# Two transformer blocks in split fp32 on one core: deviations per token, the Fourier step in two turns, and three steps moved in the order

## The chip, the cores and the metric

One core of one Trainium2 chip runs the whole program in one launch. The metric is the device time of an execution in microseconds; of several executions the median counts. The engines are TensorE (PE; its weight load is PEld), VectorE (DVE), ScalarE (ACT), GpSimd (POOL) and SyncE (SP), which issues the weight DMAs.

## The reference

A first block (attention, a recurrent mixer and four gated FFNs, two layers deep) is followed by a second block, also two layers, with a mixer and a convolutional FFN in each. There are 256 latent tokens and 256 context tokens, 1024 features, 2816 hidden features in an FFN. Layer 1 of either block needs the latent tokens alone from its queries on. What the change touches:

```
def second_block(...):
    for l in range(2):
        a = modulate(rms_norm(h, g_mix), sh1, sc1)
        h = h + gt1 * mixer(a)
        h = h + gt2 * conv_ffn(modulate(rms_norm(h, g_ffn), sh2, sc2))
    return rms_norm(h_x, g_final)

def mixer(h):
    fa = real(fft2(reshape(h @ w_fa, tokens, 4, 128)))         # over tokens and 128 features
    o  = softmax(q1 k1) v - lam * softmax(q2 k2) v             # 4 heads of 128
    db = o * rsqrt(mean(o*o, last axis) + 1e-5) * subln_g * (1 - lam_init)
    nc = neighbourhood_attention(...)                          # 8 heads of 64
    g_a, g_b, g_c = split(sigmoid(h @ w_g + b_gate), 3)
    return (g_a * (fa @ w_a) + g_b * (db @ w_b) + g_c * (nc @ w_c)) @ w_out

def conv_ffn(h):
    a, b = split(dwconv3(h @ w_up), 2)                         # 3 taps along the tokens
    return (silu(a) * b) @ w_down
```

## The kernel before

Activations lie with features on the partitions: X holds 8 chunks of 128 features x 512 tokens (latent 0 to 255, context 256 to 511). Each large product is made of three matmuls per 128x128 tile: both operands are split into a high half, rounded to fp32r, and a low half, what is left (HH and HL for activations, a pair of slots in WR for weights); hi*hi, hi*lo and lo*hi are summed in one of eight banks. Weights come in slabs of up to 1 MB into three ring buffers; `split` makes a slab's high half on ScalarE (a Copy of 128x2048) and its low half on VectorE (a subtraction), into one of three pair slots (two in the mixers of attention). The ring buffer is loaded again once the low half is done.

One list, ORDER, holds every step. Each engine's program walks through it and takes its own share of a step, so the list sets the order on every engine; semaphore waits tie them together. `woven` merges lists evenly. A planner at the end puts each slab's split as early as its pair slot allows, two slabs ahead at most; in the first group of a projection, and where ORDER says `split_next`, other rules hold. The steps that matter here, with the functions that write them:

- `lin` is a projection in groups of four output chunks with K = 8 in two slabs: `slab` (one output chunk's matmuls with one slab) and `ev` (eviction of a bank). A slab step takes 12 matmuls. `first_group` runs the first group of a projection chunk by chunk behind the norm (`times`, `mod_h`, `mod_l`, the last of which makes HL); for 512 tokens it has two halves, and for 256 tokens (the last FFN of the first block, called 11, and the conv FFN of layer 1) one.
- `lin_deep` is an FFN's second product, K = 22: `part` copies a chunk of the hidden activations to HH (ScalarE) and subtracts into HL (VectorE), eight chunks at a time in the places where the first product's operand lay. Before the first of them `warm` makes ScalarE load the Sqrt table. `part` 0 waits for the last matmul of the first product. In the conv FFN an eviction is an Identity with scale and bias on ScalarE, two taps on VectorE, a Silu on ScalarE and a product on VectorE.
- `mixer2` (second block): projections and the difference attention `da`; `da_rest`, its deviations, woven into the first fifth of the gate projection; the neighbourhood attention `na`; eight `sig` (sigmoids of the first gate, in place); the second gate woven with the Fourier step; the first, second and third mix (gate times fa @ w_a and so on, into YM); `y_parts`, which splits YM for the last projection `mo`.
- `da_rest` has per head: `hsum` (Square on ScalarE, a matmul with a 128x128 tile of ones, and scale and add on VectorE over all tokens), `hroot` (Sqrt, reciprocal) and `db_norm` (the product).
- `fourier` (l, g, sg) has two matmuls with the 128-point table, VectorE's two copies to UC (one of two buffers, by the number n = 2g + sg), four matmuls with the 256-point tables, ScalarE's copy to the high half and VectorE's subtraction. There are eight in layer 0 and four in layer 1, where all numbers are even.

In the first block `head_sq`, `head_sum`, `head_root` and `head_spread` do the same as da_rest in another form: sums per token into a few columns of one bank, root and reciprocal of these few columns, and a matmul that spreads each column over its partitions.

Of the kernel before, what the change touches and what calls it, by code (L numbers as in the profile page):

```python
# [10 lines left out]
ALU = mybir.AluOpType  # L11
ACT = mybir.ActivationFunctionType
AXX = mybir.AxisListType.X
P = 128
# [5 lines left out]
EPS = 1e-6  # L20
# [140 lines left out]
def program(nc, A, out):  # L161
    ctx = ExitStack()
    with ctx:
# [233 lines left out]
        def first_group(J):  # L397
# [7 lines left out]
            for k in range(K):  # L405
                chunk(k + 2, 0)
                ORDER.append(("slab_k", J, k // 4, k, 0))
                if halves == 2:
# [10 lines left out]
                    if k >= 6:  # L419
                        chunk(k - 6, 1)  # L420
            if halves == 2:
# [88 lines left out]
        HEAD = {"eqk": (0, 5, 0, 1.0 / 64, EPS), "kk": (40, 4, 5, 1.0, EPS), "read": (0, 4, 9, 1.0 / 64, GN_EPS)}  # L510
# [32 lines left out]
        def even_mixer(mods0, mods1):  # L543
# [14 lines left out]
            for name, w0, w1 in (("eqk", 0, 7), ("kk", 6, 14)):  # L558
                n = HEAD[name][1]
# [47 lines left out]

        def head_rstd(name, src, dst, n, width, scale, eps, group):
            for m in range(n):
                ORDER.append(("hsum", name, m, src(m), dst(m), width, scale, eps, group))  # L610
            for m in range(n):
                ORDER.append(("hroot", name, m, dst(m)))
# [141 lines left out]
        MRS = wv(XTRA, [4, 512])  # L754
# [21 lines left out]
        def mixer2(l):  # L776
# [190 lines left out]
        def tensor_program(e, q):  # L967
# [182 lines left out]
            def hsum(name, m, src, dst, width, scale, eps, group):  # L1150
                q.wait_ge(IN["cst"], ("in", "cst"))
                q.wait_ge(ACTS, ("hsq", name, m))
                o = take(("hsum", name, m))
                mm(o[:, 0:width], C(group), SQ[m % 2][:, 0:width], True, True).then_inc(
                    MM.sem, MM.mark(("hsum", name, m)))
                shut(("hsum", name, m))

# [9 lines left out]
            def head_sum(name, m):  # L1167
                o0, n, i0, *_ = HEAD[name]
# [3 lines left out]
                q.wait_ge(ACTS, ("head_sq", i0 + m))  # L1172
# [1235 lines left out]
```

## Time and profile before

| | |
|---|---|
| timed runs | 3922.23, 3925.08, 3933.41 us; median 3925.08 |
| profiled execution | 3916.84 us; its span 3915.0 us |
| mean granted clock of TensorE | 0.965 |
| TensorE, weight loads | 3598.5 us (92%), 2964.7 us (76%) |
| VectorE, ScalarE, GpSimd | 1895.7 (48%), 1388.0 (35%), 60.1 us (2%) |
| DMA | 453.93 MB, mean 116 GB/s |

A row of the timeline gives the start and the duration in us, the engine, the line of the kernel (988 is the helper of every matmul, 1209 the transposes, 1422 every activation, 1742 to 1757 VectorE's helpers), the operation, out<-in, the shape, and how many alike were merged; in brackets the engine's idle time just before and what ended it. Layer 0 of the second block's mixer runs from about 2340 to 2885 us of the span, layer 1's from about 3330 to 3685.

### The profile page before, as it was taken

What the parts mean: (1) busy time and instruction counts of PE and PEld (TensorE: products, weight loads), DVE (VectorE), ACT (ScalarE), POOL (GpSimd) and SP (SyncE); (2) the same over time, 40 slices, a digit from 0 to 9 for tenths busy, and PEclk for the clock granted to TensorE, in tenths of its full rate; (3) what the DMA queues carried; (4) which work ended last, traced back from release to release, by engine and by line L of the source; (5) the groups of instructions that cost most, each with busy time, mean ns of one, the idle gap of its engine ahead of it and who ended that gap; (6) DMA issues with size and microseconds to landing.
All of it is one profiled execution on the core that took longest, in us unless ns stands there. A gap on an engine that the chain in (4) does not pass through costs nothing.

```text
span 3915.0 us, 61954 instructions
## 1 busy us (share of the span) xinstructions
PE 3598.5 (92%) x27214; PEld 2964.7 (76%) x27214; DVE 1895.7 (48%) x3248; ACT 1388.0 (35%) x2195; POOL 60.1 (2%) x98
## 2 busy tenths in 40 slices
PE   6999999888889999999987979988999999988798
PEld 4777874777668888878756978656887778778798
DVE  2223455777754233323465444662454443564574
ACT  3213435322233233323334343442243333344453
POOL 0000000000010000000000000010000000010000
PEclk8999999999999999999998989999999999999899
DMA  5444224222243322333145542121225542233453
GB/s 188 173 164 140 76 63 145 89 99 99 88 96 96 97 92 84 119 129 123 61 162 178 185 144 76 60 60 54 87 86 180 184 159 79 97 97 108 134 178 109
DMA packets 257918, 453.93 MB, mean 116 GB/s; under 512 B 14096, under 2 KB 157584, under 8 KB 243184
## 3 DMA queue, kind: packets, MB, share of 16 engines
q1 hardware_dynamic: 253840, 441.68, 33.7%
q0 software_dynamic: 3808, 8.27, 1.3%
q8 instruction: 215, 3.52, 0.4%
q14 instruction: 55, 0.45, 0.0%
HBM read 447.24 MB, written 1.94 MB: 115 GB/s over the span
## 4 chain that ended last, share of the span: by engine, by line
PE 78%; DVE 13%; ACT 5%; DMA 2%; issue 2%; SPq 0%; POOL 0%; DVEq 0%; ACTq 0%; POOLq 0%
PE bank L988 77%; DVE WR L1742 2%; DVE W L1751 2%; DVE W L1742 2%; ACT W L1422 2%; ACT WR L1422 2%; PE bank L1209 1%; DVE W L1754 1%; DVE H L1742 1%; DVE HL L1742 1%; DVE X L1751 1%; DMA ring<-in_w_mod 1%; DMA ring<-in_w_ada 1%; DVE small L2005 1%; ACT H L1422 0%
## 5 line engine op out<-in xcount | busy, mean ns | idle before, releaser
L988 PE MATMUL bank<-HH,WR 128*128 128x512 f32 (+1 forms) x9312 | 2430.7, 348 | 94.1 <-DVE HL L1742 46.5
L988 PEld LDWEIGHTS bank<-HH,WR 128*128 128x128 f32 x9312 | 1647.8, 193 | 352.0 <-DVE HL L1742 57.9
L988 PE MATMUL bank<-HL,WR 128*128 128x512 f32 (+1 forms) x4656 | 1603.8, 344 | 0.0
L1742 DVE TENSOR_TENSOR WR<-ring,WR 128x2048 fp32r<-128x2048 f32 (+3 forms) x300 | 674.0, 2252 | 1181.1 <-ACT WR L1422 1181.1
L1422 ACT ACTIVATE WR<-ring 128x2048 fp32r<-128x2048 f32 (+3 forms) x300 | 562.5, 1881 | 1235.5 <-PE bank L988 837.5
L988 PEld LDWEIGHTS bank<-HL,WR 128*128 128x128 f32 x4656 | 898.6, 193 | 97.8 <-issue 0.7
L1422 ACT ACTIVATE W<-bank 64x256 f32<-64x256 f32 (+3 forms) x582 | 259.2, 449 | 482.1 <-PE bank L988 440.4
L988 PE MATMUL bank<-W 64*64 64x64 f32 (+5 forms) x6304 | 366.6, 252 | 59.7 <-ACT W L1422 20.4
L988 PEld LDWEIGHTS bank<-W 64*64 64x64 f32 (+3 forms) x6304 | 277.2, 144 | 152.9 <-issue 53.7
L1422 ACT ACTIVATE W<-bank,small 128x512 f32<-128x512 f32 (+2 forms) x183 | 113.0, 621 | 261.1 <-DVE small L2005 178.4
L1754 DVE COPY W<-bank 64x256 f32<-64x256 f32 (+3 forms) x352 | 135.2, 396 | 108.6 <-PE bank L988 103.9
L1742 DVE TENSOR_TENSOR W<-W,bank 128x512 f32<-128x512 f32 (+1 forms) x140 | 82.9, 597 | 180.0 <-PE bank L988 179.8
L1751 DVE SCALAR_TENSOR_TENSOR W<-bank,vec,W 128x510 f32<-128x510 f32 (+1 forms) x206 | 130.6, 634 | 79.0 <-ACT W L1422 75.2
L988 PE MATMUL bank<-ring,silc 128*32 128x512 f32 x960 | 143.3, 643 | 23.0 <-DMA ring<-in_w_mod 16.3
L988 PE MATMUL bank<-cst,W 64*64 64x64 f32 (+6 forms) x1264 | 125.6, 266 | 32.1 <-DVE W L1754 22.2
L988 PEld LDWEIGHTS bank<-cst,W 128*128 128x128 f32 (+2 forms) x1264 | 107.7, 163 | 60.1 <-DVE W L1754 24.5
L1209 PE MATMUL bank<-cst,W 128*128 128x128 f32 x432 | 77.2, 295 | 38.1 <-DVE W L1746 33.5
L1209 PEld LDWEIGHTS bank<-cst,W 128*128 128x128 f32 x432 | 48.5, 146 | 81.1 <-issue 37.4
L1422 ACT ACTIVATE W<-bank,vec 128x512 f32<-128x512 f32 (+1 forms) x136 | 83.3, 628 | 59.9 <-PE bank L988 57.9
L988 PE MATMUL bank<-WR,HH 128*128 128x512 f32 (+2 forms) x384 | 102.8, 357 | 0.0
L1422 ACT ACTIVATE H<-H,MOD 128x256 f32<-128x256 f32 x144 | 86.1, 598 | 44.4 <-DVE H L1742 44.4
L1422 ACT ACTIVATE W<-W 128x512 f32<-128x512 f32 (+2 forms) x98 | 50.1, 532 | 145.5 <-DVE W L1751 91.8
(107 smaller groups left out, 2080.2 us busy)
## 6 DMA issues: line engine op xcount, KB each, us to landing
ring<-in_ffn_in SPq DMA_DIRECT2D x176, 512.0 KB, 5.0
ring<-in_w_mod SPq DMA_DIRECT2D x72, 1024.0 KB, 5.0
ring<-in_w_in SPq DMA_DIRECT2D x52, 1024.0 KB, 5.1
ring<-in_w_ada SPq DMA_DIRECT2D x48, 1024.0 KB, 6.5
ring<-in_ffn_out SPq DMA_DIRECT2D x176, 256.0 KB, 3.6
ring<-in_w_up SPq DMA_DIRECT2D x88, 512.0 KB, 5.1
ring<-in_w_down SPq DMA_DIRECT2D x88, 256.0 KB, 3.6
ring<-in_even_w_in SPq DMA_DIRECT2D x8, 1024.0 KB, 5.1
```

What stands on the lines that cost most here:

```text
L988: return e.matmul(o, l, r, start=start, stop=stop, skip_group_check=True)
L1209: x = e.transpose(o[:, c * P:(c + 1) * P], a["P"][j % 3][0][:, c * P:(c + 1) * P], C("ident"))
L1422: return e.activation(o, i, f, **kw).then_inc(ACTS.sem, ACTS.mark(*events))
L1742: put(e.tensor_tensor(o, a, b, op), *events)
L1751: put(e.scalar_tensor_tensor(out=o, in0=a, scalar=s, in1=b, op0=op0, op1=op1), *events)
L1754: put(e.tensor_copy(o, a), *events)
L2005: put(e.tensor_reduce(neg, bank[:, lo:nk], AXX, ALU.max, negate=True), ("neg", name, i, j))
```

## The change

- `da_rest` uses the head steps of the first block: sums per token (one column per head and 128 tokens), one root and reciprocal of 16 (layer 0) or 8 columns, and a spread per head; the steps hsum, hroot, db_norm and the tile MRS go.
- `fourier` becomes `fourier_a` (first product and copies) and `fourier_b` (second product and split); a of the next number stands ahead of b of this one, and the first a ahead of the gate projection. The buffer alternates by the count in both layers.
- The eight `sig` are woven among the gate projection's steps.
- In the third mix `y_parts` of a chunk comes after the eviction of the next.
- `lin_deep` puts parts 0 and 1 ahead of the last eviction of the first product, and `warm` behind them.
- `first_group` with one half (256 tokens) gets a `split_next` at k = 5, which splits the projection's third slab there.

```diff
 def lin_deep(name, wt, src, ntok, mod, idx, norm, ready):
-    ORDER.append(("warm",))
     J = Job(name, "deep", ...)
-    for k in range(4):
+    last = max(i for i, x in enumerate(ORDER) if x[0] == "ev")
+    ORDER[last:last] = [("part", J, k) for k in range(2)]
+    ORDER.append(("warm",))
+    for k in range(2, 4):
         ORDER.append(("part", J, k))
...
 # first_group, in the loop over k
                 if k >= 6:
                     chunk(k - 6, 1)
+            elif k == 5:
+                ORDER.append(("split_next",))
...
-HEAD = {"eqk": (0, 5, 0, 1.0 / 64, EPS), ...}
+HEAD = {n: dict(at=at, n=m, i0=i0, scale=scale, eps=eps, per=per, tok=tok) for ... in (
+    ("eqk", HN[:, 0:40], 5, 0, 1.0 / 64, EPS, 2, 4), ("kk", ...), ("read", ...),
+    ("db0", small[:, 36:52], 4, 13, 1.0 / P, 1e-5, 1, 4),
+    ("db1", small[:, 36:44], 4, 17, 1.0 / P, 1e-5, 1, 2))}
...
 def da_rest():
-    head_rstd(f"db{l}", lambda m: DB[:, m, 0:nq], lambda m: MRS[:, m, 0:nq], 4, nq, 1.0 / P, 1e-5, "ones")
+    n = f"db{l}"
+    ORDER.extend([("head_sq", n, 0), ("head_sq", n, 1), ("head_sum", n, 0), ("head_sq", n, 2), ("head_sum", n, 1),
+                  ("head_sq", n, 3), ("head_sum", n, 2), ("head_sum", n, 3), ("head_root", n)])
     for h in range(4):
-        ORDER.append(("db_norm", l, h, nq))
+        ORDER.append(("head_spread", n, h))
...
-for c in range(8):
-    ORDER.append(("sig", l, c, nq))
-woven(taken(lambda: gates(l, 1, nq, "gate")),
-      [("fourier", l, g, sg) for g in range(4) for sg in range(nq // 256)])
+ns = [2 * g + sg for g in range(4) for sg in range(nq // 256)]
+ORDER.append(("fourier_a", l, ns[0]))
+turns = []
+for i, n in enumerate(ns):
+    turns += [("fourier_a", l, x) for x in ns[i + 1:i + 2]] + [("fourier_b", l, n)]
+woven(taken(lambda: gates(l, 1, nq, "gate")), turns, [("sig", l, c, nq) for c in range(8)])
...
         if step[0] == "ev":
-            ORDER.append(("y_parts", l, 4 * step[1].kw["half"] + step[3], nq))
+            c = 4 * step[1].kw["half"] + step[3]
+            if c:
+                ORDER.append(("y_parts", l, c - 1, nq))
+    ORDER.append(("y_parts", l, 7, nq))
...
 # tensor engine, head_sum and head_spread
+ones = C("blk")... if per == 2 else C("ones", 0, 1)
+for t in range(tok):
+    c = per * (tok * m + t)
+    x = mm(banks[BANK["head", name]][:, c:c + per], src[:, t * P:(t + 1) * P], ones, True, True)
...
+for t, h in pairs(tok, per):
+    c = per * (tok * m + t) + h
+    x = mm(o[w * h:w * h + w, t * P:(t + 1) * P], d["at"][:, c:c + 1].to_broadcast([P, w]), C("ident"), True, True)
...
 # vector engine, head_spread of db and fourier_a
+stt(x, x, SUB, held(key)[:, 0:n], ALU.mult, ALU.mult, ("db", int(name[2]), m), ("free", key))
...
+UC = UCS[n // (1 + l) % 2]
+if n // (1 + l) >= 2:
+    q.wait_ge(MM, ("f2", l, n - 2 * (1 + l)))
```

## Rows read from the trace of the kernel before

**Rows 1.** the page: busy time, share of the span and instructions, by engine:
```profile
PE 3598.5 (92%) x27214; PEld 2964.7 (76%) x27214; DVE 1895.7 (48%) x3248; ACT 1388.0 (35%) x2195; POOL 60.1 (2%) x98
```

**Rows 2.** the page: chain that ended last, share of the span by engine:
```profile
PE 78%; DVE 13%; ACT 5%; DMA 2%; issue 2%; SPq 0%; POOL 0%; DVEq 0%; ACTq 0%; POOLq 0%
```

**Rows 3.** who TensorE waited for, whole span: total us, times, longest us:
```profile
PE bank L988 <- DVE HL L1742: 46.5, 20, 9.3
```

**Rows 4.** two windows: length, busy us by engine, PEclk, DMA share, GB/s:
```profile
2671.80:2675.30 3.50, 3.50 (x9) 2.83 (x9) 0.00 (x0) 0.00 (x0) 0.00 (x0) 0.51 0.83 294
3710.40:3716.30 5.90, 5.90 (x28) 5.90 (x29) 4.31 (x2) 0.69 (x1) 0.00 (x0) 0.50 0.83 259
```

**Rows 5.** timeline around both layers' deviations, TensorE and VectorE:
```profile
2535.05 1.02 PE L988 MATMUL bank<-W,cst 128*128 128x512 f32 x2
2536.71 12.98 DVE L1757 RECIPROCAL W<-W 128x512 f32<-128x512 f32 x4
2554.95 0.68 DVE L1742 TENSOR_TENSOR W<-W,cst 128x512 f32<-128x512 f32 x1
2559.36 1.09 PE L1209 MATMUL bank<-cst,W 128*128 128x128 f32 x4 [10.45 <-DVE W L1746]
...
3480.64 1.09 PE L1209 MATMUL bank<-cst,W 128*128 128x128 f32 x4 [6.08 <-DVE W L1746]
```

**Rows 6.** timeline, TensorE, a norm's sums per token and its spread over partitions:
```profile
2115.78 0.60 PE L988 MATMUL bank<-cst,W 128*128 128x1 f32 x4 [0.50 <-ACT W L1422]
2117.08 0.71 PE L988 MATMUL bank<-cst,small 128*128 128x128 f32 x4 [0.69 <-DVE small L1757]
```

**Rows 7.** TensorE's waits in the gate stages 2662 to 2745 and 3545 to 3592:
```profile
PE bank L988 <- DVE W L1754: 13.8, 8, 6.7
...
PE bank L988 <- DVE W L1754: 8.4, 4, 4.2
```

**Rows 8.** timeline, ScalarE and VectorE, start of layer 0's gate stage:
```profile
2662.60 4.27 ACT L1422 ACTIVATE W<-W 128x512 f32<-128x512 f32 x8
2668.70 2.29 DVE L1742 TENSOR_TENSOR WR<-ring,WR 128x2048 fp32r<-128x2048 f32 x1 [7.12 <-ACT WR L1422]
```

**Rows 9.** timeline, third mix and output projection, layer 0 and then layer 1:
```profile
2867.21 0.50 PE L988 MATMUL bank<-HH,WR 128*128 128x512 f32 x1 [2.33 <-DVE WR L1742]
...
3649.89 0.39 PE L988 MATMUL bank<-HH,WR 128*128 128x256 f32 x1 [3.64 <-DVE WR L1742]
3656.19 1.28 ACT L1422 ACT_TABLE_LOAD   x1
3656.21 0.42 DVE L1742 TENSOR_TENSOR HL<-W,HH 128x256 fp32r<-128x256 f32 x1 [0.48 <-ACT HH L1422]
3657.49 0.20 ACT L1422 ACTIVATE small<-small 128x1 f32<-128x1 f32 x1
3661.87 0.58 PE L988 MATMUL bank<-HH,WR 128*128 128x256 f32 x1 [4.48 <-DVE WR L1742]
```

**Rows 10.** timeline, start of the two conv FFNs' second matmul:
```profile
3183.87 1.52 DVE L1751 SCALAR_TENSOR_TENSOR W<-bank,vec,W 128x510 f32<-128x510 f32 x2
3186.56 3.69 DVE L1742 TENSOR_TENSOR HL<-W,HH 128x512 fp32r<-128x512 f32 x6
3187.39 0.77 PE L988 MATMUL bank<-HH,WR 128*128 128x512 f32 x1 [9.34 <-DVE HL L1742]
...
3834.10 0.55 PE L988 MATMUL bank<-HH,WR 128*128 128x256 f32 x1 [5.69 <-DVE HL L1742]
```

**Rows 11.** timeline, end of a first group of 256 tokens, twice:
```profile
2138.06 0.39 PE L988 MATMUL bank<-HH,WR 128*128 128x256 f32 x1 [3.88 <-DVE WR L1742]
...
3705.59 5.50 ACT L1422 ACTIVATE WR<-ring 128x2048 fp32r<-128x2048 f32 x3
3710.36 0.58 PE L988 MATMUL bank<-HH,WR 128*128 128x256 f32 x1 [8.77 <-DVE WR L1742]
```

**Rows 12.** the first group's stretch, columns as in rows 4:
```profile
2120.00:2134.00 14.00, 14.00 (x96) 13.97 (x96) 5.80 (x18) 6.84 (x13) 0.00 (x0) 0.80 0.00 1
```

More of the change, by code:

```diff
@@ L509, in program @@
         HN = wv(12032, [72])
-        HEAD = {"eqk": (0, 5, 0, 1.0 / 64, EPS), "kk": (40, 4, 5, 1.0, EPS), "read": (0, 4, 9, 1.0 / 64, GN_EPS)}
+        HEAD = {n: dict(at=at, n=m, i0=i0, scale=scale, eps=eps, per=per, tok=tok) for n, at, m, i0, scale, eps, per, tok in (
+            ("eqk", HN[:, 0:40], 5, 0, 1.0 / 64, EPS, 2, 4), ("kk", HN[:, 40:72], 4, 5, 1.0, EPS, 2, 4),
+            ("read", HN[:, 0:32], 4, 9, 1.0 / 64, GN_EPS, 2, 4), ("db0", small[:, 36:52], 4, 13, 1.0 / P, 1e-5, 1, 4),
+            ("db1", small[:, 36:44], 4, 17, 1.0 / P, 1e-5, 1, 2))}
         EF_ORDER = [range(4, 8), range(0, 4), range(8, 12), range(12, 15)]
@@ L1171, in head_sum @@
                 q.wait_ge(IN["cst"], ("in", "cst"))
-                q.wait_ge(ACTS, ("head_sq", i0 + m))
-                src = X1[m] if name == "read" else SQ[(i0 + m) % 2]
-                two = C("blk").rearrange("p (a b) -> p a b", a=2)[:, :, 0]
-                for t in range(4):
-                    x = mm(banks[BANK["head", name]][:, 8 * m + 2 * t:8 * m + 2 * t + 2], src[:, t * P:(t + 1) * P],
-                           two, True, True)
-                x.then_inc(MM.sem, MM.mark(("head_sq", i0 + m)))
-                if m == n - 1:
+                q.wait_ge(ACTS, ("head_sq", i))
+                src = X1[m] if name == "read" else SQ[i % 2]
+                ones = C("blk").rearrange("p (a b) -> p a b", a=2)[:, :, 0] if per == 2 else C("ones", 0, 1)
+                for t in range(tok):
+                    c = per * (tok * m + t)
+                    x = mm(banks[BANK["head", name]][:, c:c + per], src[:, t * P:(t + 1) * P], ones, True, True)
+                x.then_inc(MM.sem, MM.mark(("head_sq", i)))
+                if m == d["n"] - 1:
                     shut(("head", name))
             def head_spread(name, m):
-                o0 = HEAD[name][0] + 8 * m
+                d = HEAD[name]
+                per, tok = d["per"], d["tok"]
+                w = P // per
                 key = ("head_b", name, m)
@@ L1557, in bar @@
                 q.wait_ge(POOLS, ("bar", n))
-            def hsum(name, m, src, dst, width, scale, eps, group):
-                if name == "kk":
-                    q.wait_ge(DVES, ("kk",))
-                elif name in ("db0", "db1"):
-                    a = "da" + name[-1]
-                    q.wait_ge(DVES, ("o", a, (m + 1) * (ATT[a]["n"] // 4) - 1))
-                if m >= 2:
-                    q.wait_ge(MM, ("hsum", name, m - 2))
-                act(SQ[m % 2][:, 0:width], src, ACT.Square, ("hsq", name, m))
-            def hroot(name, m, dst):
-                q.wait_ge(DVES, ("hvar", name, m))
-                act(dst, dst, ACT.Sqrt, ("hroot", name, m))
             def att(name, i):
@@ L1701, in read_a @@
                 q.wait_ge(DVES, ("ry", j))
-                act(X1[j], Y[:, j, :], ACT.Square, ("head_sq", HEAD["read"][2] + j))
+                act(X1[j], Y[:, j, :], ACT.Square, ("head_sq", HEAD["read"]["i0"] + j))
             def lam(l):
@@ L1938, in head_root @@
             def head_root(name):
-                o0, n, i0, scale, eps = HEAD[name]
-                v = HN[:, o0:o0 + 8 * n]
-                q.wait_ge(MM, ("head_sq", i0 + n - 1))
-                ts(v, held(("head", name))[:, 0:8 * n], scale, eps, ALU.mult, ALU.add, ("head_v", name), ("free", ("head", name)))
+                d = HEAD[name]
+                v, n = d["at"], d["n"]
+                q.wait_ge(MM, ("head_sq", d["i0"] + n - 1))
+                ts(v, held(("head", name))[:, 0:d["per"] * d["tok"] * n], d["scale"], d["eps"], ALU.mult, ALU.add, ("head_v", name),
+                   ("free", ("head", name)))
                 q.wait_ge(ACTS, ("head_r", name))
@@ L1965, in rope @@
                 tt(x, x, t, ALU.add, key)
-            def hsum(name, m, src, dst, width, scale, eps, group):
-                key = ("hsum", name, m)
-                q.wait_ge(MM, key)
-                ts(dst, held(key)[:, 0:width], scale, eps, ALU.mult, ALU.add, ("hvar", name, m), ("free", key))
-            def hroot(name, m, dst):
-                q.wait_ge(ACTS, ("hroot", name, m))
-                recip(dst, dst)
             def att(name, i):
```

73 lines of the change are left out of this document (32 added, 41 removed).

## The prediction

> **What bounds the kernel now.** I read the page first. TensorE is busy for 92% of the span [rows 1] and carries 78% of the chain that ended last, VectorE 13%, ScalarE 5% [rows 2]. Time can therefore go only where TensorE stands still or runs at its lower clock. Then I asked who TensorE waited for. The largest entry is VectorE's low parts of activations (HL), 46.5 us in 20 waits, the longest 9.3 [rows 3]: TensorE is held up in a few places, not everywhere. Then the timeline around each wait longer than 0.5 us in the places that the diff touches, and last the windows behind them: after the long waits TensorE's granted clock is 0.50 to 0.51 of full (1.2 GHz instead of 2.4) for 3.4 to 6 us of busy matmuls [rows 4] (ten such stretches; the first that bears on the change and the longest are shown), and half of each is lost beside the wait itself.
>
> All sums below are in the time of the profiled execution, 3916.84 us (span 3915.0 and 1.8 around it). It lies 8.2 us under the median of the timed runs, 3925.08; I take the difference from there.
>
> **Deviations of the difference attention (da_rest).** Before: per head a Square, one matmul with ones over all tokens, a scale-and-add, a Sqrt and a reciprocal, all on 128x512. The four reciprocals of layer 0 take 12.98 us in one piece on VectorE [rows 5], and the neighbourhood attention that follows waits behind them: TensorE stands 10.45 us in layer 0 and 6.08 us in layer 1 (256 tokens) before its first transposes [rows 5]. After: 16 (or 8) columns instead of 4 x 512, so the scale-and-add, Sqrt and reciprocal are three small operations. What is late next: the last head_spread comes just ahead of the first scores, and behind it VectorE still has its product (0.75 us in layer 0, 0.45 in layer 1) and the chain from the first bias mask to the first transposes, 2554.95 to 2559.36, 4.4 us [rows 5]. TensorE fills some 2.0 to 2.2 us of that with four score matmuls, so a wait of 3.2 us stays in layer 0, 2.7 in layer 1: 7.2 and 3.4 us gained. The root's own chain (under 1 us; the table load can be over before it) lies beside slab 0's fourth step (2.8 us or 1.4). TensorE pays for it: per head, four sums with one moving column and four spreads of 128 columns in place of one matmul of 512 (1.02 us for the pair of records) [rows 5]. Two such sums take 0.60 us, two spreads 0.71 us [rows 6]; back to back I take 0.95 and 1.05 for four, so +1.0 us per head in layer 0, +0.6 in layer 1: 4.0 and 2.4 us. The clock behind layer 1's shorter wait may hold (1.0 us). Sum: 3.2 + 2.0 = **5 us**. Bounds: if VectorE were always ready, the waits would go whole, 12; if the small matmuls cost twice as much and the waits stay at 5, minus 3.
>
> **Fourier step in two turns, sigmoids among the gates.** Before, each step put its second product right behind its first, so TensorE waited for VectorE's copies each time: 13.8 us in 8 waits in layer 0, 8.4 us in 4 in layer 1 [rows 7]. The longest, 6.7 us, has a cause of its own: ScalarE does eight sigmoids in a row (4.27 us), only then the high half of the next gate slab, and VectorE's low half (2.29 us) stands ahead of the copies [rows 8]. After: the first Fourier product goes ahead of the gates and one or two gate steps (2.76 us each at 512 tokens, 1.4 at 256) stand between a step's copies and its second product; the copies take 0.4 us each, a split ahead of them at most 2.3. In layer 1 the two buffers really alternate (before, all even numbers shared the first). The sigmoids cost ScalarE the same, in pieces of 0.55 us between evictions; it is busy for 35% of the span. Eight banks suffice: the gate group holds four, the products rotate over four and find each freed two steps earlier. So all 22.2 us go. Of the clock: two stretches of 3.4 us in layer 0 (behind the first wait [rows 4] and behind a later one) and one in layer 1, half of each, 5.2 us. Sum **27 us**. Lower bound: with one half of the small waits and none of the clock back, 18; upper 29.
>
> **Parts of y one step later (third mix).** Before, VectorE multiplies, adds, waits 0.48 us for ScalarE's copy and subtracts: 1.70 us per chunk at 256 tokens (three operations of 0.41 and that wait; one chunk of eight is shown [rows 9]), against 1.44 us of TensorE. After, the subtraction belongs to the chunk before: three operations of 0.42, some 1.25 us, and ScalarE's split of the output projection's first slab starts 2.8 us sooner; TensorE's wait of 3.64 us [rows 9] shrinks to 0.7 to 0.9. The second slab's split still has the last y part and the Sqrt table load (1.28 us) ahead of it [rows 9]. Counted through, its low half is ready at 3657.9 instead of 3661.8, so the second wait does not shrink (4.48 becomes 4.9 after the earlier start) but everything behind it comes 4.0 us sooner; one of two slow stretches goes (1.7). Layer 0: 0.7 us less per chunk, the second slab is ready at about 2861.5, before it is needed at 2864.9: the wait of 2.33 us [rows 9] goes. Sum **8 us**, bounds 4 and 10.
>
> Here a rule bears. The rows show a table load of 1.28 us at 3656.19 and the next activation at 3657.49, within 0.03 us of its end [rows 9]. The Trainium skill (ScalarE: Activation LUTs, What ACT_TABLE_LOAD costs) says that a switch costs 1283 ns plus a drain of some 1380 ns. By it the second slab would come 1.4 us later and this part would give 6.6 us; the trace agrees with the first number only, so I keep 1.28.
>
> **Deep operand's parts 0 and 1 ahead of the last eviction.** It matters where VectorE lags. In layer 0's conv, TensorE waits 9.34 us at 3187.39; VectorE starts the last chunk's eviction at 3183.87 and the first part's subtraction at 3186.56 [rows 10]. The part now stands where the eviction stood, so it starts 2.7 us sooner; ScalarE's two copies (0.54 each) come before its last Identity and the table load, so they are ready. In layer 1 (wait 5.69 [rows 10], half the width) 1.35. In the four FFNs ScalarE's table load was already hidden and VectorE is up to date: 0.8 us for the first (a mod step stands in the chain), 0.1 for each of the others. The moved eviction delays only a bank that TensorE takes seven steps later. Sum **5 us**, bounds 3 and 7: the slow clock stays, since the waits of 6.6 and 4.3 us stay long.
>
> **Third split in the first group of 256 tokens.** Before, the third slab of the input projection is split only after the first group's evictions: ScalarE does three splits from 3705.59, TensorE waits 8.77 us (conv, layer 1), 3.88 us (the last FFN of the first block) [rows 11]. While the first group multiplies (2120 to 2134), VectorE is busy 5.8 of 14 us, ScalarE 6.8, and the DMA queues move nothing: the slabs lie in the ring already [rows 12]. So the split's 1.9 + 2.3 us fit in; they push the group's last low half (HL 7) back by about 4 us, to 2130.4 and 3698.4; it is needed 1.4 us before the group ends, at 2132.7 and 3700.1 [rows 11]. What is late next: the fourth slab. In the FFN it is ready at 2138.0, TensorE is through with the third (5.8 us) at 2139.9: 3.9 us gained, and the slow stretch behind it, 1.7. In the conv it is ready only at 3710.3, behind evictions and Silu, with the third done at 3707.4: a wait of 2.9 stays, 5.8 gained, and of 5.9 us at the lower clock [rows 4] I take 2.5 off, 1.3. Sum **13 us**, bounds 8 and 17.
>
> Total: 5 + 27 + 8 + 5 + 13 = 58 us, that is 3925 - 58 = **3867 us**.
>
> **Rivals.** (a) The waits come back further on: the stretches behind them are held by ScalarE and VectorE, not by TensorE, and a third to a half of the gain returns as new short waits. For it: the waits on VectorE have many small neighbours in both attentions, and I credit every long wait to its full length. Against: behind each wait stand projections that only need slabs already split. All lower bounds: 18 + 4 + 3 + 8 - 3 = 30 us, 3895. (b) More comes back than counted: VectorE is relieved of 20 us of reciprocals, the attention starts without a wait and the clock holds behind the rest: the upper bounds, 75 us, 3850. (c) The slower side: TensorE's clock. The change puts columns of one and small products with short pauses into stretches that ran almost wholly at 2.4 GHz; if they made the granted clock fall to 1.2 GHz for good in the two gate stages (some 85 us at layer 0, 45 at layer 1), that would cost up to 130 us more. It decides from 58 us on, that is when somewhat under half of these stages runs slow: 3990 us if nearly all does. Against: every slow stretch that I looked at here starts in or behind a wait of TensorE, and the change shortens those. The Trainium skill (TensorE: Matmul & The Clock Gate, A second HAM failure mode: psum-queue depth-cycling) says that frequent micro-idles between groups of matmuls make the clock swing between its levels; by that rule it is the before version, with its eight waits in the Fourier step, that suffers, and the trace agrees as far as [rows 4] goes. (d) It doesn't do what it says: the third split is held by something and blocks ScalarE and VectorE in the first group; then HL 7 comes late and that part gives nothing, 3880 us.
>
> **Chances.** The forecast (3853 to 3882) 0.66; (a), with (d), 3882 to 3913: 0.20; (b) under 3853: 0.07; no change within 0.3%, that is 12 us, about what a measurement of this kernel can tell: 0.03; (c) or anything slower 0.04. Faster by over 0.3%: 0.93. Range for 8 in 10: 3851 to 3890, since (a) is likelier than (b).
>
> **What would show it.** Right: no reciprocal of 128x512 or 128x256 left on VectorE; TensorE waits of some 3 us ahead of the first transposes of the neighbourhood attention; no TensorE wait for VectorE's copies in the gate stages; the waits 9.34, 8.77 and 3.88 become 6.6, 2.9 and 0; the mean granted clock rises from 0.965 to about 0.97. Wrong: a wait of more than 1 us before a second Fourier product, a TensorE wait for HL inside the first group of 256 tokens, busy matmul time that grows by more than 10 us, or a slow stretch where TensorE had not waited.

## Result and profile after

The kernel after takes 3866.78 us (the median of 3858.07, 3858.30, 3875.26 and 4541.09), the one before in the same session 3924.18 us: a ratio of 0.9842, 95% interval 0.9805 to 0.9878. The execution of 4541.09 us ran at a mean granted clock of 0.74 and is left out of every comparison but this median. The forecast was 3867.0 us. A second session of the same kernel (in the experiments) gave 3854.97, 3855.11, 3858.25 and 3871.40; over the other seven the median is 3858.3. So the change is worth 62 us (by the ratio) to 66 (by these medians); the first session's median, with the execution of 4541.09 us in it, says 57.

The profiled execution is the 3875.26 one, the longest of those three. Its page, busy time and chain (to [rows 1, 2]), and TensorE's waits for VectorE's low parts (to [rows 3]):

```profile
PE 3617.2 (93%) x27294; PEld 2978.0 (77%) x27294; DVE 1872.8 (48%) x3236; ACT 1385.9 (36%) x2189; POOL 60.1 (2%) x98
PE 82%; DVE 10%; ACT 4%; DMA 2%; issue 1%; SPq 0%; POOL 0%; DVEq 0%; ACTq 0%; POOLq 0%
PE bank L995 <- DVE HL L1738: 40.6, 20, 8.2
```

The first 2110 us, in which the change touches only the parts of the FFNs' deep operands, must be kept apart from the rest. Windows of the kernel after, and then of a second profile of the same code (length, busy us of TensorE, weight loads, VectorE, ScalarE, GpSimd, then PEclk, DMA share, GB/s):

```profile
616.00:640.60 24.60, 24.60 (x82) 9.46 (x82) 7.57 (x19) 7.26 (x17) 0.00 (x0) 0.51 0.37 129
661.00:674.60 13.60, 13.60 (x49) 6.70 (x47) 7.47 (x21) 5.49 (x12) 0.00 (x0) 0.50 0.00 1
```
```profile
616.00:640.60 24.60, 23.95 (x144) 9.47 (x136) 12.46 (x33) 13.61 (x32) 0.00 (x0) 1.00 0.69 233
```

The two windows from 616 begin at the same matmuls to 0.25 us: in one execution TensorE is granted 1.2 GHz (0.51) while it is busy without a gap and gets through 82 matmuls, in the other 2.4 GHz (1.00) and 144. The window from 661 is a second such stretch of the first profile. Each begins 1.6 to 2.0 us behind a short wait (2.36 and 1.37 us), but the repetition has both waits as well and no such stretch behind them. At one mark, the start of the norm ahead of the last FFN of the first block, the profile of before stood at 2109.91 us, that of after at 2129.75, its repetition at 2110.97. So the profiled execution is 18.8 us behind its repetition before the code that matters begins: it spent 191 us at 1.2 GHz up to the mark, the repetition 137, and TensorE's idle time between 60 us and the mark is the same within 1 us (125.6 and 126.3). The stretches behind that mark, first of before, then of after (their borders are TensorE's long waits, so that the same work stands in both):

```profile
2109.91:2350.65 240.74, 210.59 (x1689) 203.93 (x1689) 112.10 (x135) 100.44 (x131) 0.92 (x1) 0.92 0.50 160
2350.65:2644.77 294.12, 268.61 (x1453) 207.35 (x1453) 166.73 (x346) 122.36 (x239) 19.57 (x32) 0.98 0.21 65
2644.77:2904.22 259.45, 242.68 (x1149) 198.39 (x1149) 102.46 (x138) 80.24 (x108) 0.00 (x0) 0.97 0.24 81
2904.22:3187.39 283.17, 272.98 (x1384) 210.14 (x1385) 144.45 (x181) 105.02 (x127) 0.00 (x0) 0.99 0.49 171
3329.72:3533.57 203.85, 188.00 (x1093) 151.28 (x1093) 122.80 (x220) 87.18 (x148) 19.52 (x32) 0.96 0.30 94
3533.57:3661.87 128.30, 111.76 (x848) 107.48 (x849) 62.33 (x93) 53.65 (x73) 0.00 (x0) 0.95 0.37 123
3687.82:3834.10 146.28, 131.82 (x1057) 131.45 (x1057) 105.64 (x151) 78.86 (x105) 0.00 (x0) 0.94 0.49 159
```
```profile
2129.75:2363.48 233.73, 207.56 (x1689) 201.50 (x1689) 112.10 (x135) 100.49 (x131) 0.92 (x1) 0.94 0.52 165
2363.48:2655.05 291.57, 274.01 (x1508) 214.44 (x1508) 151.78 (x340) 120.47 (x236) 19.63 (x32) 0.98 0.21 66
2655.05:2894.27 239.22, 238.59 (x1149) 198.00 (x1149) 102.25 (x138) 80.16 (x108) 0.00 (x0) 0.99 0.27 88
2894.27:3176.91 282.64, 273.01 (x1385) 210.14 (x1385) 141.92 (x175) 102.36 (x122) 0.00 (x0) 0.99 0.49 171
3319.22:3518.53 199.31, 188.38 (x1117) 151.99 (x1117) 115.06 (x214) 85.93 (x145) 19.52 (x32) 0.98 0.30 96
3518.53:3629.70 111.17, 106.51 (x848) 104.22 (x848) 61.79 (x93) 53.70 (x73) 0.00 (x0) 0.99 0.42 142
3655.70:3794.09 138.39, 131.06 (x1056) 130.68 (x1057) 104.24 (x148) 77.56 (x101) 0.00 (x0) 0.97 0.52 168
```

Read line against line, the lengths give 7.0 (third split), 2.6 (deviations, layer 0), 20.2 (gates, Fourier and y of layer 0), 0.5 (deep operand), 4.5, 17.1 and 7.9 us (the same of layer 1, and third split with deep operand); the rest of the program gives 1.8. In sum 61.7 us behind the mark, 1805.1 to 1743.4. The weight is in the two gate stages, and there TensorE now hardly stands still: in the third line it is busy 238.59 of 239.22 us. The repetition has 234.79, 288.70, 239.28, 282.05, 199.39, 111.31 and 138.17 us for the seven stretches: the gate stages repeat within 0.2 us, but the first two stretches move by 1.1 and 2.9 us with the clock, so the 7.0 and the 2.6 are known no better than that.

The waits named in the prediction. TensorE before the first transposes of each neighbourhood attention (to [rows 5]), the output projection of layer 1 (to [rows 9]), the two deep products (to [rows 10]) and the third split in the conv (to [rows 11]):

```profile
2568.04 0.63 PE L1211 MATMUL bank<-cst,W 128*128 128x128 f32 x4 [3.19 <-DVE W L1742]
3466.53 0.63 PE L1211 MATMUL bank<-cst,W 128*128 128x128 f32 x4 [1.46 <-DVE W L1742]
3619.44 0.38 PE L995 MATMUL bank<-HH,WR 128*128 128x256 f32 x1 [0.47 <-DVE WR L1738]
3629.70 0.39 PE L995 MATMUL bank<-HH,WR 128*128 128x256 f32 x1 [4.20 <-DVE WR L1738]
3176.91 0.77 PE L995 MATMUL bank<-HH,WR 128*128 128x512 f32 x1 [8.19 <-DVE HL L1738]
3794.09 0.35 PE L995 MATMUL bank<-HH,WR 128*128 128x256 f32 x1 [4.32 <-DVE HL L1738]
3678.72 0.58 PE L995 MATMUL bank<-HH,WR 128*128 128x256 f32 x1 [3.02 <-DVE WR L1738]
```

In the gate stages (2655 to 2740 and 3522 to 3566) no TensorE wait for VectorE's copies is left, where [rows 7] had 13.8 and 8.4 us; the waits of 3.88 [rows 11] and 2.33 us [rows 9] are gone too.

### The profile page after: what moved, and what is told of

It reads as the page before. It is cut to its first block, busy times and chain, and to the rows that moved or that the text cites. A ratio compares the mean times of both kernels' runs of the same rounds, so it can differ in the third digit from the quotient of the medians.

```text
span 3873.2 us, 62098 instructions
## 1 busy us (share of the span) xinstructions
PE 3617.2 (93%) x27294; PEld 2978.0 (77%) x27294; DVE 1872.8 (48%) x3236; ACT 1385.9 (36%) x2189; POOL 60.1 (2%) x98
## 4 chain that ended last, share of the span: by engine, by line
PE 82%; DVE 10%; ACT 4%; DMA 2%; issue 1%; SPq 0%; POOL 0%; DVEq 0%; ACTq 0%; POOLq 0%
PE bank L995 81%; DVE W L1747 2%; DVE W L1738 2%; DVE WR L1738 2%; ACT W L1426 2%; ACT WR L1426 1%; PE bank L1211 1%; DVE H L1738 1%; DMA ring<-in_w_ada 1%; DVE X L1747 1%; DVE small L1997 1%; DMA ring<-in_w_mod 1%; DVE HL L1738 1%; ACT H L1426 1%; DVE W L1750 0%
## 5 line engine op out<-in xcount | busy, mean ns | idle before, releaser
L995 PE MATMUL bank<-W 64*64 64x64 f32 (+5 forms) x6304 | 375.8, 256 | 57.3 <-ACT W L1426 20.1
L995 PE MATMUL bank<-cst,W 64*64 64x64 f32 (+6 forms) x1312 | 128.5, 262 | 10.9 <-ACT W L1426 7.6
L1997 DVE TENSOR_REDUCE small<-bank 128x1 f32<-128x512 f32 (+1 forms) x128 | 72.9, 586 | 60.9 <-PE bank L995 59.8
```

Of the source, the lines that this page charges most:

```text
L995: return e.matmul(o, l, r, start=start, stop=stop, skip_group_check=True)
L1997: put(e.tensor_reduce(neg, bank[:, lo:nk], AXX, ALU.max, negate=True), ("neg", name, i, j))
```

## Experiments

Most kernels are the changed kernel with one part undone; the last two take it further. "Tail" is the length from the mark near 2110 us to the end of the profiled execution: the change works there, and it is free of the clock in the first half, though not of the clock behind the mark. Times are medians; the changed kernel stands at 3858.3 and its tail at 1743.4 and 1741.9. Each ratio is to the kernel before in the same session, whose medians were 3924.13, 3922.82 and 3920.39 us.

```
kernel            time us   ratio to before (95%)     mark     tail
before             3924      1                        2109.9   1805.1
changed            3858.3    0.9842 (.9825 .9859)     2111.0   1741.9
one_turn           3874.83   0.9873 (.9852 .9894)     2117.7   1768.1
sig_ahead          3860.22   0.9836 (.9818 .9855)     2117.5   1742.8
turns_and_sig      3888.77   0.9912 (.9898 .9926)     2105.6   1774.2
no_third           3869.96   0.9871 (.9847 .9894)     2111.3   1759.7
old_dev            3865.81   0.9851 (.9832 .9870)     2105.7   1757.9
y_same             3865.35   0.9866 (.9849 .9882)     2108.0   1752.7
deep_behind        3862.88   0.9844 (.9830 .9857)     2112.6   1753.0
split_later        3848.68   0.9813 (.9800 .9826)     2112.3   1733.0
further            3834.51   0.9785 (.9768 .9803)     2114.3   1719.9
```

Only turns_and_sig and further lie with their whole interval outside that of the changed kernel. By the ratios one_turn is 12 us slower than it, turns_and_sig 27, no_third 11, old_dev 4, y_same 9, deep_behind 1; the differences of medians given below are 16.6, 30.5, 11.7, 7.5, 7.1 and 4.6. So a difference of times under some 10 us shows little by itself; what each part does is read from the waits and from the stage lengths in the profiles.

**The turns without the weaving undone.**
```diff
-for i, n in enumerate(ns):
-    turns += [("fourier_a", l, x) for x in ns[i + 1:i + 2]] + [("fourier_b", l, n)]
...
+pairs_ = [("fourier", l, n) for n in ns]
...
+for x in taken(lambda: woven(gs, pairs_, [("sig", l, c, nq) for c in range(8)])):
+    ORDER.extend([("fourier_a", l, x[2]), ("fourier_b", l, x[2])] if x[0] == "fourier" else [x])
```


> The changed kernel, but each Fourier step puts its second product right behind its first again, as before the change; the eight sigmoids stay among the gate steps. My theory (term B of the sum is made of two parts: the sigmoids' row ahead of the gate slab, and VectorE's copies right behind the first product): the long wait of 6.7 us in layer 0 and its counterpart of 4.2 in layer 1 stay gone (1 us each is left of them, since they too stand behind copies), the small ones come back: (13.8 - 6.7) + 1.0 = 8.1 us in layer 0 and (8.4 - 4.2) + 1.0 = 5.2 in layer 1, some 13 us of waits by TensorE for VectorE's copies, and 1.7 us of clock: about 15 us slower than the changed kernel. Rival 1 (the sigmoids were all of it): under 4 us of waits, under 4 us slower. Rival 2 (the waits come back further on anyway): the waits are back, the time is not longer by more than 4 us.

TensorE's waits in the gate stages of layer 0 and layer 1 (total, times, longest):
```profile
PE bank L994 <- DVE W L1749: 8.3, 8, 2.1
...
PE bank L994 <- DVE W L1749: 5.3, 4, 1.6
```
13.6 us of waits where my theory had 13.3, and the time is 16.6 us above the changed kernel's (12 by the ratio), with 15 expected. The two gate stages are 251.3 and 117.7 us long instead of 239.2 and 111.2, 18.6 together. The tail is 26.2 us longer, but its profile is the longest of the four executions (3887.62 us) and has 122 us at 1.2 GHz behind the mark against 92 and 96. Both rivals fall: the sigmoids were not all of it, and the time is longer by more than 4 us.

**The weaving alone undone.**
```diff
+for c in range(8):
+    ORDER.append(("sig", l, c, nq))
-woven(taken(lambda: gates(l, 1, nq, "gate")), turns, [("sig", l, c, nq) for c in range(8)])
+woven(taken(lambda: gates(l, 1, nq, "gate")), turns)
```


> The changed kernel, but the eight sigmoids stand in a row ahead of the gates again; the Fourier step keeps its two turns. My theory: with two gate steps between the copies and the second product, most of the 4.27 us of sigmoids is hidden, but the high half of the next gate slab and with it VectorE's low half come 4.3 us later in layer 0 and 2.2 in layer 1; TensorE waits 0 to 3 us for a low half or a copy in layer 0 (I take 2) and 0 to 1.5 in layer 1 (I take 0.7): 3 us slower. Rival (the sigmoids' row by itself makes the long waits, whatever the turns are): 5 to 6.7 us and 3 to 4.2 us of waits, and a stretch at the lower clock behind the first: 10 us or more slower.

No wait of TensorE for VectorE in either gate stage, time and tail as in the changed kernel (1742.8). I expected 3 us and it was nothing: with the turns in place the 4.27 us of sigmoids in a row are hidden whole. The weaving is not needed once the turns are there.

**Both undone.**
```diff
+for c in range(8):
+    ORDER.append(("sig", l, c, nq))
...
+for x in taken(lambda: woven(gs, pairs_)):
+    ORDER.extend([("fourier_a", l, x[2]), ("fourier_b", l, x[2])] if x[0] == "fourier" else [x])
```


> The changed kernel with the whole gate stage as before the change: the eight sigmoids in a row ahead of the gates, and each Fourier step's second product right behind its first. The run that undid the turns alone brought back 8.1 us of waits in layer 0 and 5.3 in layer 1; the run that undid the sigmoids' weaving alone brought back none. My theory (the two cover each other: the 6.7 and 4.2 us arise only where a second product follows at once behind copies that queue behind the low half that the sigmoids delay): 13.8 and 8.4 us of waits and slow stretches behind them, 22.2 + 5.2 = 27 us slower than the changed kernel, about 3887. Rival (the sigmoids cost nothing in the new surroundings, because something else in this stage has moved): as the run without the turns, 13.4 us of waits, about 3874.

```profile
PE bank L996 <- DVE W L1751: 13.8, 8, 6.7
...
PE bank L996 <- DVE W L1751: 8.4, 4, 4.2
```
These are [rows 7] again, to the digit. 3888.77 against 3887 expected; the layer 0 stage is 18.3 us longer than in the changed kernel (257.5 against 239.2), the layer 1 stage 12.3 (123.5 against 111.2): 30.6 us, of which 22.2 are the waits and 7.4 the clock (the stretches at 1.2 GHz in these stages grow by 14.8 us, half of which is lost). So the two parts are not additive: undoing the turns brings 13.6 us of waits, undoing the weaving none, undoing both 22.2 (by the stage lengths 18.6, 0 and 30.6 us).

**The third split undone.**
```diff
-                elif k == 5:
-                    ORDER.append(("split_next",))
```


> The changed kernel without the third split in the first group of 256 tokens. My theory: TensorE's waits of 3.88 us (last FFN of the first block) and 8.8 us (conv, layer 1, 3.02 in the changed kernel) come back, with slow stretches behind both (3.0 us): 3.9 + 5.8 + 3.0 = 13 us slower. Rival 1 (only the waits count, the clock is made up elsewhere): 9.7 us. Rival 2 (the conv's wait is set by VectorE being late from the fourth slab on, so the third slab's split gives nothing there): 4 to 6 us.

```profile
2139.43 0.39 PE L993 MATMUL bank<-HH,WR 128*128 128x256 f32 x1 [3.88 <-DVE WR L1736]
3669.89 0.58 PE L993 MATMUL bank<-HH,WR 128*128 128x256 f32 x1 [8.77 <-DVE WR L1736]
```
The waits are those of [rows 11]; the stretches they stand in are 7.1 and 6.1 us longer than in the changed kernel, 13.2 together, and the time 11.7: as forecast. Rival 2 falls by the 8.77. Rival 1 falls for the first wait, whose stretch is 3.2 us longer than the wait alone, and not for the second, whose stretch is 6.1 us longer with 5.75 us of wait: there some 0.4 us are clock, not the 1.3 taken. Against the repetition's 234.8 us for the first stretch the 7.1 would be 6.0.

**The old deviations.**
```diff
+for m in range(4):
+    ORDER.append(("hsum", n, m, DB[:, m, 0:nq], MRS[:, m, 0:nq], nq, 1.0 / P, 1e-5, "ones"))
+for m in range(4):
+    ORDER.append(("hroot", n, m, MRS[:, m, 0:nq]))
...
-    ORDER.append(("head_spread", n, h))
+    ORDER.append(("db_norm", l, h, nq))
```


> The changed kernel with the deviations of the difference attention worked out as before the change: one matmul with ones over all tokens per head, and scale-and-add, Sqrt and reciprocal on 128x512 (128x256 in layer 1). My theory: the waits ahead of the first transposes of the neighbourhood attention become 10.4 us (layer 0, 3.19 in the changed kernel) and 6.1 (layer 1, 1.46), 11.9 us more, and TensorE gets back the small matmuls, 4.0 + 2.4 us less: 5.5 us slower, 1 more for the clock. Rival 1 (VectorE's 20 us of reciprocals also hold up what follows in both attentions): 10 us or more slower, with the extra in waits behind the first transposes. Rival 2 (the small matmuls cost more than I took): within 2 us of the changed kernel.

```profile
2548.91 1.09 PE L1222 MATMUL bank<-cst,W 128*128 128x128 f32 x4 [10.45 <-DVE W L1767]
3453.91 1.09 PE L1222 MATMUL bank<-cst,W 128*128 128x128 f32 x4 [6.08 <-DVE W L1767]
```
The time is 7.5 us above the changed kernel's (4 by the ratio), 5.5 to 6.5 expected. Up to the wait in layer 0 the stretch is 4.7 us longer (209.2 against 204.6), in layer 1 3.6 (150.9 against 147.3); what follows varies with the clock by more than the question (83.9 to 88.4 us over the profiles for the first attention, which all have in common). The low rival (within 2 us) falls by these two stretches. Of the high one there is no sign: behind the first transposes the waits are those of the changed kernel, but for the last two of layer 1's attention (2.15 and 2.48 us here, 1.15 and 3.62 there, which is no more in sum). Whether a part above 6 us is more than clock can't be told.

**y parts right behind their own eviction.**
```diff
-if c:
-    ORDER.append(("y_parts", l, c - 1, nq))
+ORDER.append(("y_parts", l, c, nq))
```


> The changed kernel with each part of y worked out right behind its own eviction again (third mix), as before the change. My theory: in layer 0 the wait of 2.33 us ahead of the output projection's second slab comes back; in layer 1 TensorE's wait of 0.47 us becomes 3.6 and the one of 4.20 becomes 4.5, with one slow stretch (1.7): 2.3 + 3.2 + 0.3 + 1.7 = 7.5 us slower than the changed kernel, of which the waits are 5.8. Rival (the evictions of the last group are not delayed by ScalarE's copy, the y parts only move their waiting to another place): waits as in the changed kernel, no difference.

```profile
2837.89 0.50 PE L992 MATMUL bank<-HH,WR 128*128 128x512 f32 x1 [2.30 <-DVE WR L1735]
3603.77 0.39 PE L992 MATMUL bank<-HH,WR 128*128 128x256 f32 x1 [3.64 <-DVE WR L1735]
3615.75 0.58 PE L992 MATMUL bank<-HH,WR 128*128 128x256 f32 x1 [4.49 <-DVE WR L1735]
```
All three waits are those of [rows 9] to 0.03 us; 7.1 us slower (9 by the ratio), 7.5 expected. The gate stages with their y parts are 2.6 and 5.1 us longer. The rival falls by the waits.

**Deep operand's parts behind the last eviction.**
```diff
-ORDER[last:last] = [("part", J, k) for k in range(2)]
 ORDER.append(("warm",))
-for k in range(2, 4):
+for k in range(4):
```


> The changed kernel with the deep operand's warm step and parts 0 to 3 behind the last eviction, as before the change. In the changed kernel TensorE waits 8.19 us ahead of the conv's second product in layer 0, where I had forecast 6.6. My theory: the part's move gives its 2.7 us there, and the missing 1.6 us are lost by a split whose weights' DMA landed later against TensorE's end (it stands ahead of the last evictions on ScalarE and VectorE): then this kernel waits 8.2 + 2.7 = 10.9 us there, and in layer 1 4.3 + 1.4 = 5.7; with 0.8 for the first FFN some 5 us slower. Rival (the move is worth only 1.2 us in layer 0, the DMA plays no part): 9.3 us of wait there, 3.4 us slower in all.

**The changed kernel again.**

> The changed kernel itself once more, for the spread of its times: its profiled execution took 3875.3, two others 3858.1 and 3858.3. Theory: the 17 us between them are the granted clock in stretches that the change does not touch (the profile of the longer one shows 1.2 GHz for 23.9 and 13.7 us in the modulation products near 617 and 661, where TensorE did not wait); so the waits of this profile are the same to 0.1 us as those of the last one, and a shorter span goes with a higher mean clock (0.969 to 0.971 at 3856 us, 0.963 at 3873). Rival: the waits themselves differ between executions by several us, from DMAs that land at other times.

The two are read together. SyncE's loads, ScalarE's split ahead of the last evictions, and TensorE's wait, in the kernel before, the changed kernel, its repetition, and the kernel with the parts behind (for the first two the wait is shown above):
```profile
3166.21 6.02 SPq L2304 DMA_DIRECT2D ring<-in_w_down  x12
3171.76 1.92 ACT L1422 ACTIVATE WR<-ring 128x2048 fp32r<-128x2048 f32 x1 [4.33 <-DMA ring<-in_w_down]
```
```profile
3156.88 6.02 SPq L2295 DMA_DIRECT2D ring<-in_w_down  x12
3163.95 1.92 ACT L1426 ACTIVATE WR<-ring 128x2048 fp32r<-128x2048 f32 x1 [6.47 <-DMA ring<-in_w_down]
```
```profile
3142.84 1.92 ACT L1426 ACTIVATE WR<-ring 128x2048 fp32r<-128x2048 f32 x1 [5.48 <-DMA ring<-in_w_down]
3155.79 0.77 PE L995 MATMUL bank<-HH,WR 128*128 128x512 f32 x1 [7.18 <-DVE HL L1738]
```
```profile
3146.13 1.92 ACT L1424 ACTIVATE WR<-ring 128x2048 fp32r<-128x2048 f32 x1 [5.47 <-DMA ring<-in_w_down]
3161.76 0.77 PE L993 MATMUL bank<-HH,WR 128*128 128x512 f32 x1 [9.87 <-DVE HL L1736]
3785.20 0.55 PE L993 MATMUL bank<-HH,WR 128*128 128x256 f32 x1 [5.69 <-DVE HL L1736]
```
The split starts when its weights land. Call its lead the time by which that comes before the end of TensorE's last matmul of the first product (wait's end less wait: 3168.72, 3148.61, 3151.89). The lead is 4.77, 5.77 and 5.76 us, and wait plus lead is 12.96, 12.95 and 15.63 us; in the profile of before it was 9.34 + 6.29 = 15.63, and in six other kernels with the parts ahead, whose leads run from 4.71 to 5.89, it is 12.95 each time. So the wait follows that DMA one to one, and the move of the parts is worth 15.63 - 12.95 = 2.68 us, 2.7 forecast; my 10.9 us for this kernel took the late landing of one execution for the rule. The change did not delay the issue: SyncE's row starts 11.84 us before TensorE's end in the kernel before and in the changed one (3178.05 and 3168.72), and it took 5.55 and 7.07 us from there to the split. What differs is how long the loads took; why, the profiles do not say. In layer 1 the move gives 5.69 - 4.31 = 1.4. The time is 4.6 us above the changed kernel's, with 5 expected, but the ratios, 0.9844 and 0.9842 in the same session, do not tell the two kernels apart: this part is shown by its waits alone.

For the spread, theory and rival both hold in part: the spans go with the clock (3852.9 us at 0.970, 3873.2 at 0.963), and apart from this DMA all waits behind the mark agree between the two profiles within 0.4 us.

**The split behind the evictions.** The lead suggests a cure, which the change does not have.
```diff
+late = [JOBS[j].slabs[1][0] for j in ("c0o", "c1o")]
...
+                    if todo[0] in late and not (step[1].kind == "deep"):
+                        break
```


> The changed kernel, but the split of the second weight slab of the conv's second product (both layers) is placed at that product's own steps instead of ahead of the last evictions of its first product. My theory (a split that waits for its DMA holds up the evictions behind it): ScalarE's first eviction starts when its bank is ready, 3160.5 to 3161 in the changed kernel's time instead of 3165.77; the chain of four evictions then runs with TensorE's 2.7 us per chunk, and the wait of 8.19 us in layer 0 becomes 1 to 2 us; the slow stretch behind it goes (3.4 us). In layer 1 the DMA is not late there, but the low half (2.29 us) stands ahead of the first eviction: 4.32 becomes 2 to 2.5, with a new wait of up to 1 us for the second slab. Together 9 to 12 us faster than the changed kernel. Rival 1 (the evictions are held by their own chain between ScalarE and VectorE, not by the split): both waits stay within 1 us, no change. Rival 2 (the split is needed early): a new wait of 3 to 5 us for the second slab in both layers, gain under 4 us.

ScalarE's first eviction, VectorE's parts and TensorE's waits in it:
```profile
3142.05 0.78 ACT L1429 ACTIVATE W<-bank,vec 128x512 f32<-128x512 f32 x1 [2.33 <-PE bank L998]
...
3150.87 1.29 DVE L1741 TENSOR_TENSOR HL<-W,HH 128x512 fp32r<-128x512 f32 x2
...
3151.71 0.47 PE L998 MATMUL bank<-HH,WR 128*128 128x512 f32 x1 [0.75 <-DVE HL L1741]
3767.37 0.36 PE L998 MATMUL bank<-HH,WR 128*128 128x256 f32 x1 [2.14 <-DVE HL L1741]
```
The eviction now waits for its bank and not for a DMA, 8.9 us before TensorE's end at 3150.96 instead of 2.95. The waits are 0.75 and 2.14 us, the time 9.6 us shorter (8.0 in the same session), there is no new wait for the second slab (rival 2), and rival 1 is refuted by the first of these rows.

**Three more places of the same kind.** The edit above stays; these come on top, all in one run.
```diff
-elif k == 5:
+elif k in (5, 7):
...
-("head_sum", n, 3), ("head_root", n)])
+("head_sum", n, 3), ("nmasked", l, 0), ("nmasked", l, 1), ("head_root", n)])
...
-ORDER.append(("warm",))
+n_mo = len(ORDER)
 lin(f"mo{l}", "add", A["w_out"][l], chunks(0, 8), KD, nq, ready=f"y{l}", mod=l, idx=2, norm=f"nc{l}")
+ORDER.insert(n_mo + 2, ("warm",))
```


> The changed kernel with four more edits: the split of the second slab of the conv's second product at that product's own steps (by itself it made the waits of 7.2 and 4.3 us 0.75 and 2.14), the split of the fourth slab too inside the first group of 256 tokens, the Sqrt table load ahead of the output projection moved behind that projection's first two steps, and the first two bias masks of the neighbourhood attention ahead of the deviations' root. My theory, from 3848.7: the fourth slab ends the wait of 3.0 us (conv, layer 1) and part of the clock behind it, 3 to 4; the table load behind the two steps takes 1.3 off the wait of 4.2; the masks take 0.7 and 0.5 off the waits of 3.2 and 1.5: together 6 to 7 us, 3842. Rival: the fourth split in the first group pushes the low halves of the group's own operand back, a new wait of 2 us or more for HL there in the last FFN of the first block or the conv, and the sum is 0 to 2 us.

```profile
3599.06 0.39 PE L999 MATMUL bank<-HH,WR 128*128 128x256 f32 x1 [2.70 <-DVE WR L1742]
3754.99 0.44 PE L999 MATMUL bank<-HH,WR 128*128 128x256 f32 x1 [2.15 <-DVE HL L1742]
```
3834.51 us, 2.15% under before and 0.6% under the changed kernel: the version to keep. It is 14.2 us below the one before it (11 by the ratios), where I expected 6 to 7; its tail is 13.1 us shorter. The waits moved as expected (3.02 us of the fourth slab gone, 4.20 to 2.70, 3.19 to 2.33, 1.46 to 0.44: 6.4 us), and the rest goes with the clock: behind the mark the stretches at 1.2 GHz shrink from 89.0 to 72.3 us, half of that is 8.3. Of these 16.7 us, 7.5 lie in layer 0's attention and come and go in the changed kernel too (7.4 us in one profile, 0.4 in the other), so up to 3.7 us may be chance in the profile; the four times (3829.13 to 3844.55) spread by more. The rival's new wait for HL is not there.

## Why the prediction was right, step by step

**Fourier and sigmoids** (27 us, the largest term). Right in size, a little low: 30.5 by the medians, 27 by the ratios, 30.6 by the stage lengths. The waits are 22.2 to the digit; the clock gave 7.4 us instead of 5.2, since I credited only stretches that I had listed. Right for a partly wrong reason: I gave the woven sigmoids a share in removing the 6.7 us wait. The runs show that either edit removes most of it (1.25 us is left without the turns, nothing without the weaving) and that the turns alone remove everything.

**Third split** (13 us): 13.2 by the stretches, 11.7 by time. The forecast waits of 0 and 2.9 became 0 and 3.02. The clock was taken at 1.7 and 1.3 us and gave 3.2 (2.2 against the repetition) and 0.4.

**y parts** (8 us): 7.1. Forecast waits of 0.7 to 0.9 and 4.9 were 0.47 and 4.20.

**Deviations** (5 us): 7.1 in the stretches from before to after, 8.3 in those of the run without them, 7.5 by its median and 4 by its ratio. The wait left in layer 0 was 3.19 (3.2 forecast), in layer 1 1.46 instead of 2.7. The chain that I carried over from layer 0 was right, 4.41 us from the first mask at 3462.12 to the transposes at 3466.53; what I had wrong is what TensorE does meanwhile. I had 2.2 us of score matmuls, but in layer 1 only half of them stand there, then a gate step of 1.6 us, then the other half, 3.8 us together from 3461.26 on:
```profile
3461.26 1.13 PE L995 MATMUL bank<-W 64*128 64x512 f32 x4
3462.12 0.69 DVE L1738 TENSOR_TENSOR W<-W,cst 128x512 f32<-128x512 f32 x1
3463.93 1.13 PE L995 MATMUL bank<-W 64*128 64x512 f32 x4
```
TensorE's price was right: timeline of the changed kernel, two heads' spreads in layer 0,
```profile
2557.34 1.95 PE L995 MATMUL bank<-cst,small 128*128 128x128 f32 x16
```
0.98 per head, where I had 1.05.

**Deep operand** (5 us): the move itself is right at 2.68 and 1.4. What the prediction got wrong is that the wait in layer 0 would therefore be 6.6: it was 8.19, 7.18 in the repetition, because the wait also follows the landing of the weights that the split ahead of the evictions waits for. The prediction took that landing as it was in the one profile of before, 6.29 us ahead of TensorE's end; in the nine later profiles with the split in that place it was 4.71 to 5.89. The row that says so, ScalarE's wait at 3171.76, was in the trace of before, and I did not look at it since TensorE's wait was put down to VectorE. In the first FFN the wait for HL (2.01 us before, 2.00 with the parts behind) is gone, but TensorE's wait for ScalarE just ahead of it is 2.46 us instead of 1.45 and 0.93, so 1.0 or 0.5 us are gained where I had 0.8. From the profile of before to that of after the whole term gave 1.15 + 1.37 + 1.0 = 3.5 us, to the repetition 4.5.

**The rivals.** (a), the waits return further on: no; the waits that the change did not touch are the same within 0.1 us, but for 2.54 that became 3.62 and 2.20 that became 1.15 at the end of layer 1's attention, and a new one of 0.6 (0.9 in the repetition) in layer 0's conv. (b), the upper bounds: nearer than I thought, with 62 to 66 us of the 75. (c), the small products lower the clock: no, the gate stages' granted clock rose from 0.97 and 0.95 to 0.99. The Trainium skill (TensorE: Matmul & The Clock Gate, A second HAM failure mode: psum-queue depth-cycling) has frequent micro-idles as a cause of swings; the run with eight waits of up to 2.1 us back in layer 0 agrees weakly, 3.6 us more at 1.2 GHz in that stage. (d): no.

**The signs.** Of those of "right" two did not come as written: the 9.34 us became 8.2 and not 6.6, and layer 1's wait ahead of the transposes 1.5 and not some 3. The others did (the mean granted clock was 0.963 in the profiled execution and 0.970 in the repetition). Two of those of "wrong" came as well, in the profiled execution. TensorE's busy time grew from 3598.5 to 3617.2 us, by more than 10; in the repetition it is 3596.6, so that was the clock and not the small matmuls. And there are slow stretches that no wait accounts for, those from 616 and 661 us, in code that the change does not touch. Neither sign tells a price of the change from a slower clock elsewhere, so neither should have been read from one profile.

The median matched to 0.2 us by luck: with the 4541.09 us in it, it falls halfway between 3858.30 and 3875.26. Against 3858.3 the forecast is 9 us too slow, that is 58 us of gain where 62 to 66 were measured.

## What to carry to other kernels

Where a product is fed by copies of its own first half, put other matmuls between the two; that alone may hide what stands in the other engines' queues, so try the rest of the edit without it. Where TensorE waits for VectorE, follow VectorE's and ScalarE's queues back to whether an instruction there waits for a DMA: a prepared weight that is not needed yet, placed ahead of an eviction that is, passed its full lateness on here. Compare profiles stage by stage between waits that both have, never by the span alone.

## What was not expected of the hardware

The same code ran the same small matmuls of the first block at 0.51 in one execution and 1.00 in another, with TensorE busy throughout in the slow one and equally busy just before (13.64 of 16 us in both, with the same wait of 2.36 us); the twelve profiles' marks lie between 2105.6 and 2129.8 us. Of the 20.3 us between the two profiled executions of the changed kernel, 18.8 lie ahead of the mark, and I found no cause. Four waits that came back with a part undone repeat within 0.01 us of the kernel before (10.45, 8.77, 6.71, 3.88); the one that hangs on a DMA moves by 1.2 us. VectorE's reciprocal took 0.25 us on 128x16 where the four on 128x512 took 12.98 [rows 5]:
```profile
2551.46 0.25 DVE L1753 RECIPROCAL small<-small 128x16 f32<-128x16 f32 x1 [0.28 <-ACT small L1426]
```
